# Depthwise taps of a conformer convolution on TensorE as plain fp32 products: no split of u and taps, 15 taps there instead of 13, one pair of output weights loaded later

## What is computed

```python
def conformer_conv_module(h, w1, b1, dw_w, dw_b, ln_g, ln_b, w2, b2):
    u = h @ w1 + b1                          # w1 1024 x 2048
    a, gt = jnp.split(u, 2, axis=-1)
    u = a * jax.nn.sigmoid(gt)               # 256 x 1024
    u = causal_dwconv(u, dw_w) + dw_b        # y_t = sum_k w_k u_(t-30+k), 31 taps, each channel by itself
    u = jax.nn.silu(layernorm(u, ln_g, ln_b))
    return u @ w2 + b2                       # w2 1024 x 1024
```

## Time and profile before

| | us |
|---|---|
| median of 3 executions | 1079.04 (1078.93 to 1079.52) |
| span of the profiled execution | 1077.1 |
| TensorE matmuls busy in it | 975.7 |
| VectorE busy | 852.5 |
| ScalarE busy | 542.5 |
| first matmul of block 4 to the first of its output product | 734.99 to 845.38 |

### The profile page before, as it was taken

One profiled execution on the slowest core, in us unless ns is written; L12 is line 12 of the kernel. 1 busy time (PEld: TensorE's weight loads), 2 busy tenths in 40 slices (PEclk: granted clock), 3 DMA queues, 4 the chain that ended last, 5 costly groups with the idle time before them and its releaser, 6 DMA issues.

```text
span 1077.1 us, 19816 instructions
## 1 busy us (share of the span) xinstructions
PE 975.7 (91%) x6740; PEld 897.5 (83%) x6740; DVE 852.5 (79%) x1354; ACT 542.5 (50%) x1013; POOL 69.2 (6%) x114
## 2 busy tenths in 40 slices
PE   3539997899999988998699999998998889999997
PEld 2539995899999978997699999987997679999996
DVE  6518998888887869677688887878999679987875
ACT  2325444444444456555344444447998545545542
POOL 3010002000000020111400000011000010000001
PEclk9769998899999989999699999998998889999998
DMA  9789996499999966555089999994340257766630
GB/s 342 164 216 324 331 327 188 135 322 324 309 306 314 288 206 198 164 158 166 5 263 315 315 308 313 313 309 122 105 131 1 79 156 255 233 191 182 190 119 39
DMA packets 259749, 234.96 MB, mean 218 GB/s; under 512 B 7849, under 2 KB 209314, under 8 KB 259706
## 3 DMA queue, kind: packets, MB, share of 16 engines
q1 hardware_dynamic: 256256, 226.52, 68.5%
q0 software_dynamic: 2208, 6.37, 2.7%
q10 hardware_dynamic: 1242, 1.51, 0.4%
HBM read 231.75 MB, written 2.62 MB: 218 GB/s over the span
## 4 chain that ended last, share of the span: by engine, by line
PE 67%; DVE 16%; DMA 6%; issue 5%; ACT 3%; SPq 2%; POOL 1%; DVEq 0%; POOLq 0%; ACTq 0%
PE work L477 39%; PE Y L490 20%; DVE wlo L1132 3%; DMA raw<-in_moba_w_qkv 3%; DVE acc L1144 3%; SPq L248 2%; DVE mix L1509 2%; PE work L650 2%; PE Y L753 2%; DMA ada_raw<-in_ada_w 1%; DVE acc L1155 1%; DVE xs L1180 1%; PE work L539 1%; DMA raw<-in_ada_w 1%; PE work L513 1%
## 5 line engine op out<-in xcount | busy, mean ns | idle before, releaser
L1132 DVE TENSOR_TENSOR wlo<-raw,whi 128x1024 fp32r<-128x1024 f32 x286 | 347.1, 1221 | 115.3 <-ACT whi L838 114.2
L477 PE MATMUL work<-h_hi,whi 128*128 128x256 f32 x1440 | 409.3, 284 | 12.4 <-DVE h_lo L1192 12.2
L477 PE MATMUL work<-h_lo,whi 128*128 128x256 f32 x1440 | 406.3, 282 | 0.0
L477 PE MATMUL work<-h_hi,wlo 128*128 128x256 f32 x1440 | 406.2, 282 | 0.0
L838 ACT ACTIVATE whi<-raw 128x1024 fp32r<-128x1024 f32 x286 | 298.7, 1055 | 156.7 <-PE work L477 66.3
L477 PEld LDWEIGHTS work<-h_hi,whi 128*128 128x128 f32 x1440 | 275.4, 191 | 17.8 <-issue 14.4
L477 PEld LDWEIGHTS work<-h_lo,whi 128*128 128x128 f32 x1440 | 274.7, 191 | 3.1
L477 PEld LDWEIGHTS work<-h_hi,wlo 128*128 128x128 f32 x1440 | 275.6, 191 | 0.0
L1144 DVE SCALAR_TENSOR_TENSOR acc<-ada_raw,csil,acc 128x512 f32 (+1 forms) x256 | 191.1, 746 | 6.4 <-DMA ada_raw<-in_ada_w 4.0
L490 PE MATMUL Y<-whi,ab_hi 128*128 128x512 f32 x328 | 106.4, 405 | 0.6 <-DVE ab_lo L1252 0.6
L490 PE MATMUL Y<-wlo,ab_hi 128*128 128x512 f32 x328 | 103.3, 396 | 0.0
(11 more groups left out here) (187 smaller groups left out, 1163.3 us busy)
## 6 DMA issues: line engine op xcount, KB each, us to landing
ada_raw<-in_ada_w SPq DMA_DIRECT2D x88, 512.0 KB, 6.9
raw<-in_ffn_w_in SPq DMA_DIRECT2D x88, 512.0 KB, 7.3
ada_raw<-in_mod_w SPq DMA_DIRECT2D x48, 512.0 KB, 6.6
raw<-in_ffn_w_out SPq DMA_DIRECT2D x44, 512.0 KB, 5.1
raw<-in_f_up_w SPq DMA_DIRECT2D x44, 512.0 KB, 3.9
raw<-in_moba_w_qkv SPq DMA_DIRECT2D x24, 512.0 KB, 9.0
raw<-in_diff_w_qkv SPq DMA_DIRECT2D x24, 512.0 KB, 4.9
raw<-in_a_pw_w SPq DMA_DIRECT2D x24, 512.0 KB, 5.4
```

Source lines behind the costliest of these rows:

```text
L477: mm = pe.matmul(dst, w[:, u, ws], h[:, k, :], start=(k == 0 and m == 0), stop=(k == KT - 1 and m == 2))
L1132: dve.tensor_tensor(wlo[:, u, :], raw[:, u, :], whi[:, u, :].bitcast(F32), ALU.subtract).then_inc(lo[u], 1)
```

## The change

`NP` goes from 13 to 15: VectorE keeps 16 taps. Taps and u are no longer split. The diagonals are plain fp32 and lie in `raw[:, 6:8, :]`, and each tap is one plain fp32 matmul with `upad` itself. The copies to `u_hi`, the subtractions to `u_lo`, the split of the taps ahead of the block and the copy L1485 are gone, and so are their semaphores; `conv` waits for `act_done` (u is written) instead of `ulo`. Since the diagonals now lie in `raw` of units 6 and 7, the load of the first weights of these units, `pw2_pair(1, 3, ...)`, is moved from the end of block 3 to behind the block's other loads, after a wait for the last diagonal, and ahead of `pw2_pair(2, ...)` and all that follows on that queue.

```diff
--- before.py
+++ after.py
 CONV = 31
-NP = 13
+NP = 15
 EPS, LN_EPS = 1e-6, 1e-5
...
         a_hi, a_lo = ab_hi[:, :, 0:S], ab_lo[:, :, 0:S]
-        u_hi, u_lo = ab_hi, ab_lo
 
...
         convT = head_bias[:, :, 0:S]
-        tap_hi = head_bias[:, :, S:S + CONV]
-        tap_lo = head_bias[:, :, S + 32:S + 32 + CONV]
-        tap_parts = head_bias[:, :, S:S + 64].rearrange("p t (w c) -> p t w c", w=2)[:, :, :, 0:NP]
 
...
 
-        diag = [w[:, 6:8, :].rearrange("p u (m n) -> p (u m) n", n=P) for w in (whi, wlo)]
+        diag = raw[:, 6:8, :].rearrange("p u (m n) -> p (u m) n", n=P)
 
...
         pad_zero, tap_seq, conv_done = sem("pad_zero"), sem("tap_seq"), sem("conv_done")
-        thi, tlo = sem("taps_hi_done"), sem("taps_lo_done")
-        uhi, ulo = sem("u_hi_done"), sem("u_lo_done")
         diag_done, diag_used, part_done = sem("diag_done"), sem("diag_multiplied"), sem("part_done")
...
                         units(5, (0, 1), 0, 1)
+                    sp.wait_ge(diag_used, KT * NP)
+                    pw2_pair(1, 3, USE[4][3])
                     pw2_pair(2, 2, USE[4][2] + 1)
...
                             pw2_pair(0, 2, USE[4][2])
-                            pw2_pair(1, 3, USE[4][3])
                         ada_block(s // 2 + 1, NBLK - 3)
...
                     T = i * 2 + j
-                    pe.wait_ge(ulo, T + 1)
+                    pe.wait_ge(act_done, T + (fb + 1))
                     need(pe, conv_done, T - 1)
...
                         pe.wait_ge(diag_done, T * NP + (m + 1))
-                        for n, (w, u) in enumerate(((0, u_hi), (0, u_lo), (1, u_hi))):
-                            mm = pe.matmul(Y[:, j, 0:S], diag[w][:, m, :], u[:, j, m:m + S],
-                                           start=(m == 0 and n == 0), stop=(m == NP - 1 and n == 2))
-                        mm.then_inc(diag_used, 1)
+                        pe.matmul(Y[:, j, 0:S], diag[:, m, :], upad[:, j, m:m + S], start=(m == 0),
+                                  stop=(m == NP - 1)).then_inc(diag_used, 1)
 
...
                 for j in range(2):
-                    act.wait_ge(used[6 + j], USE[4][3])
-                act.wait_ge(cols_ready, 2)
-                act.activation(tap_hi.bitcast(F32R), cols[:, ADW:ADW + CONV * KT]
-                               .rearrange("p (c t) -> p t c", t=KT), ACT.Copy).then_inc(thi, 1)
+                    act.wait_ge(lo[6 + j], USE[4][3])
 
...
                     act.wait_ge(used[2 + j], i + (nb + 1))
-                    act.wait_ge(taps_ready, i * 6 + (3 * j + 3))
+                    act.wait_ge(taps_ready, i * 4 + (2 * j + 2))
                     if not start:
...
                         prep(2 + j, i + (nb + 1))
-                    act.wait_ge(act_done, F + 1)
-                    need(act, diag_used, T * NP - NP)
-                    act.activation(u_hi[:, j, :], upad[:, j, :], ACT.Copy).then_inc(uhi, 1)
                     for m in range(NP):
...
                             act.wait_ge(diag_used, T * NP + (m + 1 - NP))
-                        for w in range(2):
-                            d = act.activation(diag[w][:, m, :], ident[:], ACT.Copy,
-                                               scale=taps[:, j, 36 + w * NP + m:37 + w * NP + m])
-                        d.then_inc(diag_done, 1)
+                        act.activation(diag[:, m, :], ident[:], ACT.Copy,
+                                       scale=taps[:, j, m:m + 1]).then_inc(diag_done, 1)
 
...
                 bias = cols[:, PW1B:PW1B + 3 * KT].rearrange("p (c t) -> p c t", t=KT)
-                dve.wait_ge(thi, 1)
-                dve.tensor_tensor(tap_lo, adw.rearrange("p c t -> p t c"), tap_hi, ALU.subtract).then_inc(tlo, 1)
                 dve.memset(upad[:, :, 0:CONV - 1], 0.0).then_inc(pad_zero, 1)
-                dve.wait_ge(tlo, 1)
                 dve.wait_ge(pad_zero, 1)
...
 
+                    need(dve, diag_done, T * NP - NP)
                     dve.tensor_scalar(taps[:, j, 0:CONV].rearrange("p (c t) -> p c t", t=1),
...
                                       bias[:, :, bass.ds(T, 1)], 1.0, None, ALU.mult).then_inc(taps_ready, 1)
-                    need(dve, diag_done, T * NP - NP)
-                    dve.tensor_scalar(taps[:, j, 36:36 + 2 * NP].rearrange("p (t w c) -> p t w c", t=1, w=2),
-                                      tap_parts[:, bass.ds(T, 1), :, :], 1.0, None, ALU.mult).then_inc(taps_ready, 1)
                     if more:
                         prep(j, i + (nb + 1))
-                    dve.wait_ge(taps_ready, i * 6 + (3 * j + 3))
+                    dve.wait_ge(taps_ready, i * 4 + (2 * j + 2))
                     dve.wait_ge(gate_done, F + 1)
...
                     dve.wait_ge(act_done, F + 1)
-                    dve.wait_ge(uhi, T + 1)
-                    dve.tensor_tensor(u_lo[:, j, :], u, u_hi[:, j, :].bitcast(F32), ALU.subtract).then_inc(ulo, 1)
                     n = T * (CONV - NP)
```

More of the change, by code:

```diff
@@ L1022, in step @@
                     if s == 5:
-                        act.wait_ge(taps_ready, i * 2 + (3 * KT + j + 1))
+                        act.wait_ge(taps_ready, i * 2 + (2 * KT + j + 1))
                         act.activation(gate[:, j, :], work[:, 2 * j, 0:S], ACT.Identity, scale=taps[:, j, 4:5],
@@ L1403, in step @@
                         gt, ut = gate[:, j, :], act32[:, j, :]
-                        dve.wait_ge(taps_ready, t1 + 3 * KT)
+                        dve.wait_ge(taps_ready, t1 + 2 * KT)
                         dve.wait_ge(cv_g0, t1)
```

## The result

| kernel | median us (lowest to highest), executions |
|---|---|
| before | 1079.52 (1078.93 to 1082.19), 5 |
| changed | 1085.8 (1083.8 to 1090.07), 5 |

The ratio is 1.0054 with a 95% interval of 1.0035 to 1.0073: 5.8 us slower (3.8 to 7.9). It isn't the quotient of the two medians, which lie 6.3 us apart; the same holds for the ratios of the experiments.

The account below looks back on a forecast made before the run. VectorE bounds block 4 at 11.09 us a step; after the change TensorE does at 12.70. TensorE's summed work ends its convolutions at 836.06 instead of 830.44: 1079.04 + 5.6 = 1084.7 us, range 1082.0 to 1088.2.

Parts of the forecast that it names:

- The price of a plain tap: Block 4's convolutions: one plain fp32 matmul of 256 columns with its own weights takes 0.436 us on TensorE.
- The rival with four full passes: Block 4's convolutions: each of four passes costs a whole split matmul, 0.471 us a tap, time 1088.9 us; chance 0.06.
- the one with cheap records: Block 4's convolutions: plain records as close as split matmuls, 0.236 us a tap, VectorE leading, time 1069 us; chance 0.03.
- TensorE's step: Block 4, per step: weights product 5.66, convolution 6.54 and `mean_sum` 0.50 make 12.70 us after the change.
- conv(0) starts where it starts now ... nothing waits there: Start of block 4: the first convolution still begins at 746.78 us, behind two weights products.
- no half clock before 836: Sign in the changed profile: TensorE is not granted 1.2 GHz before 836 us.
- then pays some 3 us for the half clock, and both of these go: Last convolution of block 4: TensorE's idle wait for the last u and some 3 us at 1.2 GHz both vanish.
- eight times the growth of a step: Block 4: 8 x 1.6 = 13 us, from the step's growth 11.09 to 12.70; the forecast difference was less, +5.6 us.
- VectorE's forecast step: Block 4, per step: without two taps and u_lo, VectorE needs 9.94 us instead of 11.09.
- u every 12.7 us from the third step on: Sign in block 4: the instruction making u, once a step, comes every 12.7 us from the third step on.
- The moved loads: Tail of block 4: later weights' loads for units 6 and 7 land within ScalarE's idle time and cost nothing.
- -1.1, -0.4 and -1.7: Lower bounds in us on the forecast: plain tap's price, `mean_sum` at 0.44, and the tail's clock; lower end given as 1082.3.

Follow-up runs that it names:

- e5: Kernel before plus 24 unread split matmuls of 256 columns on TensorE ahead of the last convolution: 1080.86 against 1080.52 us, ratio 1.0005.
- e1: Changed kernel with 13 plain fp32 taps on TensorE instead of 15: 1079.59 us against 1080.44 for the kernel before, ratio 0.9987.
- e8: Changed kernel measured again, unaltered: 1088.35 us against 1080.52 for the kernel before, ratio 1.0068.
- e4: Kernel before with only the weights' load of units 6 and 7 moved behind the last diagonal: 1080.98 against 1080.44 us, ratio 0.9999.
- e9: Kernel before (13 split taps) plus 7 unread matmuls at the start of blocks 1 to 5: 1076.6 against 1080.09 us, ratio 0.9970.
- e7: Changed kernel with 13 plain taps plus 7 unread matmuls at the start of blocks 1 to 5: 1074.06 us against 1080.52 before, ratio 0.9940.
- e6: Changed kernel with 13 plain taps plus unread split matmuls in TensorE's gaps behind the convolutions: 1083.34 us against 1080.52 before, ratio 1.0029.

## Why the prediction was right

It gave 1084.7 us in 1082.0 to 1088.2, and the time is 1085.8. Its bound, its direction and its main mechanism hold: TensorE takes the lead of block 4 and the block lasts as long as TensorE's own work.

- **The price of a plain tap**, 0.436 from a line between rows of 128 and 512 columns, measured 0.432 (6.48 / 15). The rival with four full passes (0.471) falls, and so does the one with cheap records (0.236). The Trainium skill's four passes (FP8 and Floating Point Precision, section TensorE Precision Notes) agree with this trace as far as the time goes: the prediction's sum for them was 0.437. The trace itself shows two records for a product, 0.216 apart, and not the passes.
- **TensorE's step**, 12.70, measured 12.56; `mean_sum` 0.43 and not 0.50: the row had a short wait for VectorE ahead of it, and in the changed kernel's chain there is none. From the first convolution to the end of the last the sum had 89.3 us, measured 88.1 (753.30 to 841.42). This term was 1.2 us too long.
- **"conv(0) starts where it starts now ... nothing waits there"** failed, by 1.2 us. In the changed kernel's two profiles, and in five of the seven others without filler there, half clock reaches into the first weights products (741.4 to 744.8 in the first profile, so the sign "no half clock before 836" was not met), 13.0 us instead of 11.8. The kernel before can have that too and doesn't feel it (e5: 13.03 and a block of 110.38). With TensorE in the lead it counts. The forecast had this term at nothing, and it was cancelled by the 1.2 us too much in the term above. That was luck, so 5.6 in the sum and 5.7 in the block are less of a proof than they look.
- **"then pays some 3 us for the half clock, and both of these go"** was wrong. e5 took the half clock away and the block kept its length. The last convolution was then held by ScalarE's diagonals, and its `combine` by VectorE. The sum did not use the 3 us, only its explanation did. That 5.6 is less than eight times the growth of a step needs no clock: the block before lasts as long as VectorE's whole sum, with 9.8 us of its own behind the last u, and after the change as long as TensorE's (see e1).
- **VectorE and ScalarE**: both got the room that was forecast. The first two distances between the u of the changed kernel are 9.91 and 9.74 us, where 9.94 was VectorE's forecast step, and the last four are 12.57, TensorE's step. So the mark, u every 12.7 us from the third step on, came one step later than forecast; the average of all seven is 11.50 (e8) and says nothing about who leads at the end.
- **The moved loads** at nothing: e4 shows it alone (0.9999, block 110.37 against 110.39), and the tail's chain in the changed kernel is the old one shifted, half clock over L508 and all (3.41 us in both).

The range was added up wrongly at its lower end: -1.1, -0.4 and -1.7 make 1081.5 and not 1082.3. The measured time lies far from both.

Not settled: why half clock reaches into the first product of block 4 in some executions and not in others (in that of the kernel before it lasted from 726.7 to 733.5, and the first product began at 734.99), and how much of the difference in each execution is that chance. The run-to-run spread of 6 us looks like it, since the blocks ahead differ by such pieces between two executions of one kernel, but no run here shows it by itself.

## What to carry to other kernels

When three engines are level, add up each engine's own work for the new split before moving anything: here the last two taps cost TensorE 0.86 us a step, which the room gained on ScalarE and VectorE could not give back; with the plain form the block became 1.0 us shorter at 13 taps (whole time 0.9987, up to 1.0000) and 5.7 longer at 15. An engine that becomes the bound also begins to pay for stalls that another engine used to cover. A slow stretch at the end of a chain is only worth its time if nothing else ends with it: try it with the stall taken away before booking it.

## What the runs showed of the hardware

- Records of plain fp32 matmuls of 256 columns, each with its own weights, stand 0.216 us apart at full clock, two to a product, with no gap for the weights' loads between them. Split matmuls of the same width stand 0.118 apart, so three of these (0.353) are cheaper than one plain product (0.432).
- Seven unread matmuls of 128 columns in the gap ahead of a block's first product (blocks 1 to 5) gave 3.5 us of the whole time back (e9), and together with 13 plain taps 6.5 (e7). Matmuls put between and behind products with one row did not keep the clock up: it stood at 0.50 from 835.9 to 846.0 with TensorE busy throughout, and the block was 3.6 us longer (e6).
